# A streaming encoder step with a mixture of experts: gate and up matrices loaded whole, in rows of 16 KB, into buffers on multiples of 128 bytes

## What is computed

```
xn = rms_norm(x, norm2_g)
... router: top group of 4, then top 2 of its 8 experts; combine[n, e] are the weights
for e in range(N_EXPERTS):
    hdn = silu(xn @ w_gate[e]) * (xn @ w_up[e])       # w_gate[e], w_up[e]: 1024 x 512
    out = out + combine[:, e:e+1] * (hdn @ w_down[e])  # w_down[e]: 512 x 1024
y = rms_norm(x + out, final_norm_g)
```

## Time and profile before

| what | value |
|---|---|
| median of 3 runs | 850.46 us (848.34 to 850.73) |
| the profiled execution | 847.72 us |
| its span, first to last instruction | 845.2 us |
| PE (TensorE matmul) busy | 777.2 us, 92% |
| DVE, ACT, POOL busy | 51%, 38%, 31% |
| moved by DMA | 249.98 MB, mean 296 GB/s |
| mean granted TensorE clock | 0.981 |

### The profile page before, as it was taken

How to read it: one execution, slowest core, us unless ns; L and a number is a source line. 1 busy time by engine, 2 the same in 40 slices (tenths; PEclk the granted TensorE clock), 3 DMA queues, 4 the chain that set the end, 5 groups by cost and what they waited for, 6 DMA issues and landing times.

```text
span 845.2 us, 21580 instructions
## 1 busy us (share of the span) xinstructions
PE 777.2 (92%) x8655; PEld 593.2 (70%) x8656; DVE 427.1 (51%) x1142; ACT 323.2 (38%) x559; POOL 258.5 (31%) x129
## 2 busy tenths in 40 slices
PE   3999999999999999999999989999899879989964
PEld 3999999999999999874555555555555545555532
DVE  4046978899994334144444433445333324334424
ACT  5333666655335833152332322322323213322224
POOL 3845699978576778300000000000000000000000
PEclk9999999999999999989999999999999999999997
DMA  7734343424444845974799999999999999999993
GB/s 253 228 101 150 100 125 125 150 92 144 152 167 150 299 140 214 329 320 147 307 415 419 421 421 421 419 420 421 422 420 419 421 421 422 420 420 420 422 420 153
DMA packets 53171, 249.98 MB, mean 296 GB/s; under 512 B 6599, under 2 KB 6599, under 8 KB 28561
## 3 DMA queue, kind: packets, MB, share of 16 engines
q1 hardware_dynamic: 49760, 246.95, 74.0%
q10 hardware_dynamic: 3377, 2.57, 1.3%
HBM read 246.76 MB, written 2.75 MB: 295 GB/s over the span
## 4 chain that ended last, share of the span: by engine, by line
PE 61%; DMA 21%; DVE 11%; ACT 3%; issue 2%; SPq 1%; POOL 1%; ACTq 0%; DVEq 0%
PE bank L1402 25%; DMA piece<-in_exp_w_up 20%; PE bank L1571 12%; DVE bank L1053 7%; PE bank L1600 7%; PE bank L1522 4%; PE bank L1559 4%; PE bank L1400 4%; PE bank L1587 1%; DVE sq L1115 1%; DMA raw<-in_w_in 1%; PE bank L1529 1%; SPq L548 1%; PE bank L1469 1%; PE bank L1463 1%
## 5 line engine op out<-in xcount | busy, mean ns | idle before, releaser
L602 POOL TENSOR_TENSOR w_lo<-raw,w_hi 128x2048 fp32r<-128x2048 f32 x40 | 184.9, 4624 | 76.5 <-ACT w_hi L721 76.4
L1571 PE MATMUL bank<-piece,xe 128*32 128x256 f32 x2816 | 168.7, 391 | 32.4 <-DMA piece<-in_exp_w_up 26.4
L1571 PEld LDWEIGHTS bank<-piece,xe 128*32 128x32 f32 x2816 | 97.2, 112 | 98.2 <-issue 48.0
L1402 PE MATMUL bank<-x_hi,w_hi 128*128 128x384 f32 x448 | 152.6, 341 | 1.2 <-POOL w_lo L602 1.1
L1402 PE MATMUL bank<-x_hi,w_lo 128*128 128x384 f32 x448 | 151.0, 337 | 0.0
L1402 PE MATMUL bank<-x_lo,w_hi 128*128 128x384 f32 x448 | 150.4, 336 | 0.0
L1053 DVE SCALAR_TENSOR_TENSOR bank<-ub,vec,bank 128x256 f32<-128x256 f32 (+1 forms) x416 | 137.1, 414 | 0.0
L721 ACT ACTIVATE w_hi<-raw 128x2048 fp32r<-128x2048 f32 x40 | 76.5, 1916 | 84.1 <-PE bank L1402 72.5
L1284 DVE SCALAR_TENSOR_TENSOR silu_and_hid<-bank,small,silu_and_hid 64x256 f32<-64x256 f32 x44 | 21.5, 489 | 170.3 <-ACT silu_and_hid L902 170.3
L1600 PE MATMUL bank<-piece,hidT 128*32 128x256 f32 x1408 | 94.2, 384 | 5.4
L1402 PEld LDWEIGHTS bank<-x_hi,w_hi 128*128 128x128 f32 x448 | 83.9, 187 | 2.3 <-POOL w_lo L602 1.3
(11 more groups left out here) (231 smaller groups left out, 983.7 us busy)
## 6 DMA issues: line engine op xcount, KB each, us to landing
piece<-in_exp_w_down SPq DMA_DIRECT2D x64, 1024.0 KB, 26.7
piece<-in_exp_w_gate SPq DMA_DIRECT2D x64, 1024.0 KB, 25.9
piece<-in_exp_w_up SPq DMA_DIRECT2D x64, 1024.0 KB, 27.0
raw<-in_w_in SPq DMA_DIRECT2D x28, 1024.0 KB, 5.2
raw<-in_w_out_a SPq DMA_DIRECT2D x4, 1024.0 KB, 5.1
raw<-in_w_out_b SPq DMA_DIRECT2D x4, 1024.0 KB, 5.3
raw<-in_w_o SPq DMA_DIRECT2D x4, 1024.0 KB, 5.0
out<-n_out SPq DMA_DIRECT2D x3, 512.0 KB, 3.3
```

Of the source, the lines that this page charges most:

```text
L602: pool.tensor_tensor(w_lo[u % NW][:, :, :], raw[u % NW][:, :, :], w_hi[u % NW][:, :, :].bitcast(F32), ALU.subtract).then_inc(lo_ready, 1)
L1402: ins = pe.matmul(b, wp[:, k % UK, cols], xp[:, k, :], start=start, stop=stop)
L1571: last = pe.matmul(GU[q * T:(q + 1) * T, :], xe[:, k, :], wide(pairs[q // 2], k)[:, q % 2 * QE:(q % 2 + 1) * QE], start=(k == 0), stop=(k ...
```

## The change

Gate and up are loaded as whole matrices. `w_gu` gives partition p eight rows that follow each other, so a load is 2 MB in 128 rows of 16 KB. The contraction's blocks are cut to match: block k holds the rows with index k modulo 8 (`by_row`, `norm2_by_row`), where they were k modulo 4 within a half. `SETS` is renumbered so that the two pieces of gate and of up are neighbours with an even first number, and `matrix` names them as one buffer. Down stays in two halves.

On TensorE the two parts become one: it waits for both whole matrices, does 64 matmuls and counts up `gate_up_done`; `gate_up_half` is gone. On SP, `expert_weights` waits for `gate_up_done` once, issues the two matrices, and then down's halves as before. The first loads are re-ordered by hand for the new buffers.

`small` shrinks from 48 to 32 columns and `norm2_by_row` moves, with a few small vectors, into `few` behind `halves`. With that, `halves` begins at byte 31,488, a multiple of 128 (and of 256).

```diff
     HALF = 512
-    SETS = (((15, 16), (17, 18), (20, 9)), ((10, 11), (12, 1), (2, 0)),
-            ((4, 7), (5, 8), (3, 6)), ((13, 14), (19, 21), (22, 23)))
+    SETS = (((16, 17), (10, 11), (18, 9)), ((0, 1), (4, 5), (8, 19)),
+            ((2, 3), (6, 7), (12, 13)), ((14, 15), (20, 21), (22, 23)))
+    assert all(a % 2 == 0 and b == a + 1 for s in SETS for a, b in s[0:2])
...
         iota = sb("iota", [P, T])
-        small = sb("small", [P, 48])
-        norm2_by_row = sb("norm2_by_row", [P, KB])
-        same_at = nc.sbuf_base - 4 * (2 * KB * N + 4 * N + P + T + 48 + KB)
+        small = sb("small", [P, 32])
+        same_at = nc.sbuf_base - 4 * (2 * KB * N + 4 * N + P + T + 32)
...
         halves_at = nc.sbuf_base
+        assert halves_at % 128 == 0
         halves = sb("halves", [P, HALVES * 2048])
+        few = sb("few", [P, 24])
+        norm2_by_row, mark, zero = few[:, 0:KB], few[:, 8:14], few[0:1, 14:18]
+        own_slot, slot_coef, second_sums = few[:, 18:19], few[:, 19:20], few[:, 20:20 + NT]
...
         squares = at("squares", [P, HALF], F32, halves_at + UNIT * SETS[0][1][1])
-        assert SETS[0][0][1] == SETS[0][0][0] + 1
+        matrix = {s[c][0]: at(f"matrix{s[c][0]}", [P, 4096], F32, halves_at + UNIT * s[c][0]) for s in SETS for c in range(2)}
...
         down_rank = late("down_rank", [P, NE])[:, :]
-        mark = small[:, 36:36 + 6]
-        zero = small[0:1, 31:35]
-        own_slot = small[:, 45:46]
-        slot_coef = small[:, 46:47]
...
         xe_ready = sem("xe_ready")
-        gate_up_half = sem("gate_up_half")
...
                 "Wo": w_o.rearrange("l (k p) c -> p (l k) c", p=P)}
-        w_gu = {0: w_gate.rearrange("l e (h p j) c -> (l e) h p (j c)", h=2, p=P),
-                1: w_up.rearrange("l e (h p j) c -> (l e) h p (j c)", h=2, p=P)}
+        w_gu = {0: w_gate.rearrange("l e (p j) c -> (l e) p (j c)", p=P), 1: w_up.rearrange("l e (p j) c -> (l e) p (j c)", p=P)}
...
-        RJ = KB // 2
...
-            return t.rearrange("p (h q j) -> p h j q", h=2, q=P)
+            return t.rearrange("p (q j) -> p j q", q=P)
         def wide(pair, k):
-            return piece[pair[k // RJ]][:, :].rearrange("p (j c) -> p j c", j=RJ)[:, k % RJ, :]
+            return matrix[pair[0]][:, :].rearrange("p (k c) -> p k c", k=KB)[:, k, :]
...
-            def first_weights(e, c, h):
-                n = SETS[e][c][h]
-                sp.dma_start(piece[n][:, :], (w_dn if c == 2 else w_gu[c])[e, h]).then_inc(weights_in[n], 16)
-            TAPS_USED = {32: (0, 0), 33: (1, 0), 34: (0, 1), 35: (1, 1)}
+            def first_matrix(e, c):
+                n = SETS[e][c][0]
+                sp.dma_start(matrix[n][:, :], w_gu[c][e]).then_inc(weights_in[n], 16)
+            def first_down(e, h):
+                n = SETS[e][2][h]
+                sp.dma_start(piece[n][:, :], w_dn[e, h]).then_inc(weights_in[n], 16)
+            TAPS_USED = 32
...
             for u in range(UNITS):
-                if u == 30:
-                    first_weights(0, 2, 0)
...
                 sp.dma_start(raw[u % NW][:, :, :], w[:, k0:k0 + UK, c0:c0 + HALF]).then_inc(unit_in[u % NW], 16)
-                if u in TAPS_USED:
+                if u == TAPS_USED:
...
                     sp.wait_ge(tails_ready, 2 + 4 * KB)
-                    first_weights(0, *TAPS_USED[u])
+                    first_matrix(0, 0)
+                if u == TAPS_USED + 2:
+                    first_down(0, 0)
             sp.wait_ge(grp_done, CHUNK_END[X_LO_USED])
-            first_weights(0, 2, 1)
+            first_down(0, 1)
             sp.wait_ge(grp_done, CHUNK_END[NCH - 3])
-            first_weights(1, 0, 0)
-            first_weights(1, 0, 1)
-            first_weights(1, 1, 0)
-            sp.wait_ge(lo_ready, UNITS - 2)
-            first_weights(1, 1, 1)
-            sp.wait_ge(lo_ready, UNITS - 1)
-            first_weights(1, 2, 0)
+            first_matrix(0, 1)
             sp.wait_ge(lo_ready, UNITS)
-            first_weights(1, 2, 1)
+            first_matrix(1, 0)
             sp.wait_ge(grp_done, CHUNK_END[NCH - 2])
-            first_weights(2, 0, 0)
-            first_weights(2, 0, 1)
             sp.wait_ge(half_done, NCH)
-            first_weights(2, 1, 0)
-            first_weights(2, 1, 1)
+            first_matrix(1, 1)
+            first_down(1, 0)
             sp.wait_ge(grp_done, len(GROUPS))
-            first_weights(2, 2, 0)
-            first_weights(2, 2, 1)
-            first_weights(3, 0, 0)
-            first_weights(3, 0, 1)
+            first_matrix(2, 0)
+            first_matrix(2, 1)
+            first_down(2, 0)
+            first_down(2, 1)
+            first_matrix(3, 0)
             sp.wait_ge(aux_done, aux("logit", NT - 1) + 1)
-            first_weights(3, 1, 0)
+            first_down(1, 1)
...
             sp.wait_ge(combined, 1)
-            first_weights(3, 1, 1)
-            first_weights(3, 2, 0)
-            first_weights(3, 2, 1)
+            first_matrix(3, 1)
+            first_down(3, 0)
+            first_down(3, 1)
...
-                for c, h in ((0, 0), (1, 0), (0, 1), (1, 1), (2, 0), (2, 1)):
-                    n = SETS[side][c][h]
-                    used = (down_half, down_done) if c == 2 else (gate_up_half, gate_up_done)
-                    sp.wait_ge(used[h], last_item)
-                    src = w_dn if c == 2 else w_gu[c]
-                    sp.dma_start(piece[n][:, :], src[bass.ds(e, 1), h, :, :].rearrange("e p x -> p (e x)"))\
+                sp.wait_ge(gate_up_done, last_item)
+                for c in range(2):
+                    n = SETS[side][c][0]
+                    sp.dma_start(matrix[n][:, :], w_gu[c][bass.ds(e, 1), :, :].rearrange("e p x -> p (e x)"))\
+                      .then_inc(weights_in[n], 16)
+                for h, done in enumerate((down_half, down_done)):
+                    n = SETS[side][2][h]
+                    sp.wait_ge(done, last_item)
+                    sp.dma_start(piece[n][:, :], w_dn[bass.ds(e, 1), h, :, :].rearrange("e p x -> p (e x)"))\
...
             act.dma_start(rw[:, :, NG:R], expert_w.rearrange("l (k p) g -> p (l k) g", p=P)).then_inc(rw_in, 16)
-            act.dma_start(norm2_by_row[:, :].rearrange("p (h j) -> p h j", h=2),
-                          norm2_g.rearrange("l (h p j) -> p (l h) j", h=2, p=P)).then_inc(rw_in, 16)
+            act.dma_start(norm2_by_row, norm2_g.rearrange("l (p j) -> p (l j)", p=P)).then_inc(rw_in, 16)
...
-                act.activation(x_rows[:, i, :].rearrange("p (h j q) -> p h j q", h=2, j=RJ), by_row(x_tok[:, i, :]),
+                act.activation(x_rows[:, i, :].rearrange("p (j q) -> p j q", j=KB), by_row(x_tok[:, i, :]),
...
                     act.wait_ge(weighted, 2 * n + 1)
-                at_col = (16, 42)[h] + i
+                sums = (small[:, 16:16 + NT], second_sums)[h]
                 act.activation(squares[:, :], total(i, h)[:, :], ACT.Square, scale=1.0 / ROOT_D,
-                               accum_out=small[:, at_col:at_col + 1]).then_inc(ssq_ready, 1)
+                               accum_out=sums[:, i:i + 1]).then_inc(ssq_ready, 1)
...
                 dve.wait_ge(ssq_ready, 2 * NT + 2 * n + 2)
-                dve.scalar_tensor_tensor(small[:, 20 + i:21 + i], small[:, 16 + i:17 + i], 1e-6, small[:, 42 + i:43 + i],
+                dve.scalar_tensor_tensor(small[:, 20 + i:21 + i], small[:, 16 + i:17 + i], 1e-6, second_sums[:, i:i + 1],
...
                 pe.wait_ge(xe_ready, i + 1)
-                for part, done in enumerate((gate_up_half, gate_up_done)):
-                    pe.wait_ge(weights_in[pairs[0][part]], filled)
-                    pe.wait_ge(weights_in[pairs[1][part]], filled)
-                    for k in range(part * KB // 2, (part + 1) * KB // 2):
-                        for q in range(TILES):
-                            last = pe.matmul(GU[q * T:(q + 1) * T, :], xe[:, k, :],
-                                             wide(pairs[q // 2], k)[:, q % 2 * QE:(q % 2 + 1) * QE],
-                                             start=(k == 0), stop=(k == KB - 1))
-                    last.then_inc(done, 1)
+                pe.wait_ge(weights_in[pairs[0][0]], filled)
+                pe.wait_ge(weights_in[pairs[1][0]], filled)
+                for k in range(KB):
+                    for q in range(TILES):
+                        last = pe.matmul(GU[q * T:(q + 1) * T, :], xe[:, k, :],
+                                         wide(pairs[q // 2], k)[:, q % 2 * QE:(q % 2 + 1) * QE],
+                                         start=(k == 0), stop=(k == KB - 1))
+                last.then_inc(gate_up_done, 1)
```

## The result

The changed kernel takes **846.46 us** (median of 6 runs, 844.61 to 847.10). The kernel before, run beside it, takes 850.87 us (6 runs, 848.34 to 852.11). The ratio is 0.9947, with a 95% interval from 0.9932 to 0.9961: faster by 4.4 us, with 3.3 to 5.8 us inside the interval. The forecast was 849.6 us with a range of 841.5 to 855.5, so the time lies within the range. But it is not the likeliest case that came true: -0.9 us was forecast for it, and the result stands nearer to where rival A put it (844.6 us).

The account below looks back on a forecast made before the run. It took one full stream of expert weights from 421.07 us to the last up matrix, plus TensorE's tail, as the bound. Terms -4.9 + 1.7 + 1.5 + 0.8 = -0.9 us gave 849.6 us on the median's scale, range 841.5 to 855.5.

Parts of the forecast that it names:

- the likeliest case: Whole kernel: the forecast itself, -0.9 us in sum, 849.6 us on the scale of the medians, chance 0.43.
- rival A: Weight stream: alignment counts as well, every packet loses some 6 to 11 ns; 844.6 us, chance 0.32.
- What bounds the kernel: Second half: one unbroken stream of weights, full from 421.07 us, sets the end, followed by TensorE's work after it.
- Length of the stream, -4.9 us: Loads of 27 experts: 16 fewer packets per expert and engine, each 11.5 ns fixed, make the stream 4.9 us shorter.
- Rival B: Stream and waits: 16 KB packets run no faster and coarser waits stay, +4.9 us, 855.3 us, chance 0.20.
- The 2 KB stretch: Queue at 302 to 310 us: 87.5 ns per 2 KB packet, set against 315.6 ns at 8 KB to price packets.
- I take 0 for the alignment: Weight buffers 96 bytes past a multiple of 128: moving them was priced at 0, with -14.9 us as the bound.
- Start, +1.7 us: Second refill on SP: waiting for the whole gate-up starts the full stream 1.7 us later.
- 64 matmuls after the last landing, +1.5 us: Last item on TensorE: all 64 matmuls follow the landing, 3.45 us instead of 1.93, so +1.5 us.
- Clock, +0.8 us: Last gate-up: a 6 us wait in one piece makes a TensorE clock drop likelier, +0.8 us, bounds 0 and 3.3.
- From the profile to the median: Whole kernel: 2.7 us, the median's distance above the profiled execution, added to 846.8 us to give 849.6 us.
- Rival C, ACT's copies: Ahead of the router: token copies reading with a 32-byte step delay its chain, +3 us, 852.6 us, chance 0.05.

Follow-up runs that it names:

- e2: The changed kernel with clamped item bounds, its weight buffers put back 96 bytes past a multiple of 128; 849.88 us, ratio 1.0012 to the kernel before.
- c_before: Control: the kernel before with the item bounds that TensorE loads clamped at 0; 850.99 us, ratio 1.0020 to the kernel before.
- e1: c_before with only small tiles moved, so that the buffers begin on a multiple of 128 bytes; 846.0 us, ratio 0.9961 to the kernel before.
- e4: c_after with gate and up rows laid out for 8 KB packets, still in 2 MB loads; 850.91 us, ratio 1.0019 to the kernel before.
- c_after: Control: the changed kernel with the item bounds that TensorE loads clamped at 0; 846.63 us, ratio 0.9965 to the kernel before.
- e3: c_before with coarse waits alone, all four gate and up pieces waited for and let go together; 854.58 us, ratio 1.0049 to the kernel before.
- e5: c_after with gate and up rows laid out for 4 KB packets, still in 2 MB loads; 859.34 us, ratio 1.0115 to the kernel before.
- e6: c_after with the buffers 64 bytes past a multiple of 128; 848.39 us, ratio 0.9982 to the kernel before.
- f1: c_after with first refills of sets 0 and 1 and the last expert's gate and up by halves; 843.32 us, ratio 0.9919 to the kernel before.

## Why the prediction was right and where it failed

**What bounds the kernel: right.** One stream from the second refill to the last up matrix, then a tail. The packet experiments move the end by what they add to the stream, 3.95 us of stream for 4.3 us of time and 12.05 for 12.7.

**Length of the stream, -4.9 us: right in kind, the packets' part a little large.** The stream became 5.1 to 5.4 us shorter, but packets are only 3.6 to 4.3 us of it, 8.4 to 10.0 ns each instead of 11.5; the rest is alignment. That the total came out so near to -4.9 is luck: a price of packets that was too large stood in for an alignment that was put at 0. The 2 KB stretch overstated the price, by what wasn't tried. Rival B's extreme, 16 KB packets no faster, is refuted. But its tipping point of 9.3 ns, below which the coarse waits cost more than the packets bring, lies within what was measured: without the alignment the change would be about worth nothing, as e2 is (1.1 us under c_before, the ratios' intervals overlap). The Trainium skill (DMA: Bandwidth & Descriptors, Anatomy of one DMA, for DMAs that GpSimd issues) gives each DMA about 2 us of fixed cost; on SP's queue here e1 with 1 MB loads and e4 with 2 MB loads stream alike, so if there is such a cost the queue hid it, as the prediction took it. (The 26 us that it gives for a load in flight are 27.0 in the row that it names; nothing hangs on it.)

**"I take 0 for the alignment": this step failed.** It is worth 0.8 to 1.5 us in the stream, some 1 ns a packet, far from the bound of 11.5 ns. And it is worth 1.8 to 1.9 us in TensorE's matmuls, where the prediction didn't look at all: it treated the place of the buffers as a matter of packets, though the split weights lie behind the same tiles and move with them. By medians the two kernels with one edit each say more, 5.0 us (e1 against c_before) and 3.3 us (c_after against e2), while the rows account for 3.4 and 2.7 us (1.9 + 1.5 and 1.9 + 0.8). What remains, 1.6 and 0.6 us, is within what these comparisons can tell, and one profile a kernel doesn't settle it. Rival A was right that alignment counts as well. Its mechanism, 6 to 11 ns on every packet, was not what happened, so that its time (844.6 us) came nearer than the forecast's was luck.

**Start, +1.7 us: right.** 1.74 us between the profiles. **64 matmuls after the last landing, +1.5 us: right**; e3 pays start and end together, 3.6 us by medians and 2.5 by ratios, and there is no starvation.

**Clock, +0.8 us: not borne out by the averages.** The drop was argued from a wait of 6 us in one piece; in the changed kernel the waits came out at 3.7 and 3.9 us. In the profiled pair the tail's 3.23 us are 1.71 for the first half of the matmuls (3.64 less 1.93) and 1.5 for the clock: the drop costs 1.5 us (5.14 us against the 3.64 us that such a group takes at full clock on this timeline), and in c_after 2.7. But it is not new: c_before pays 1.7 in its last half and 1.2 in the gather behind it, e1 1.3 and 0.5. Over after, c_after, e2, e3, e4, e5 and e6 the loss is 1.9 us on average (1.5, 2.7, 1.7, 1.7, 2.5, 1.7, 1.3, all in the gate-up), over before, c_before and e1 it is 1.6 (0, 2.95, 1.8). The difference is 0.3 us, too little to tell from nothing with three executions on one side. A tail without any drop was seen in one of the three kernels that take the last gate-up by halves, in none of the seven that take it whole, and in f1, which takes it by halves.

**From the profile to the median.** I added 2.7 us to the sum, the distance of the median before from its profiled execution, as though it were a constant of the measurement. It was luck of that one execution: its tail is 2.95 us shorter than c_before's (21.27 against 24.22), all of it clock (1.71 in the half, 1.24 in the gather). On the scale of the profiles the forecast of -0.9 us is close to the -1.2 that came; on the scale of the medians it is 3.5 us off. The terms as measured add up better: -1.8 for the mixer, -5.3 for the stream, +1.7 for the later refill, and +2.0 after the last up matrix (24.85 us on average in the seven kernels with the coarse form at the end, against 22.82 in the three with the fine one) are -3.4, against -4.4 by medians. The pair of profiles hid this because in it the mixer's 1.9 us were given back before the stream began. The first items, before and then after:

```profile
391.37 4.20 PE L1571 MATMUL bank<-piece,xe 128*32 128x256 f32 x64
...
400.94 3.64 PE L1571 MATMUL bank<-piece,xe 128*32 128x256 f32 x64
```

```profile
390.62 4.94 PE L1565 MATMUL bank<-matrix,xe 128*32 128x256 f32 x64
...
400.94 3.64 PE L1565 MATMUL bank<-matrix,xe 128*32 128x256 f32 x64
```

The first gate-up starts 0.75 us earlier and takes 0.74 us longer, at lower clock, so the second one starts at the same 400.94. The other 1.2 us went in the router ahead of it. But alignment is not what does this. In e1, with the same alignment, the second gate-up starts at 398.72, and the mixer's gain is kept. From the end of the mixer to the second gate-up (by the chain) it is 36.5 to 36.7 us in before, c_before, e1 and e2, 37.2 in e6 and 38.3 to 38.8 in the other six, e3 with buffers 96 past among them. Whether that is chance of an execution or comes with the coarse form, which all of the six have in the first sets (but e2 and e6 as well), one profile a kernel doesn't show. The medians speak for chance: e3's 3.6 us are filled by the later refill and the tail (1.7 + 2.0) without it.

**Rival C, ACT's copies: refuted.** With a step of 32 bytes they take about what they took with 16, 2.12 and 2.05 us against 2.04 and 2.08. The rule of the Trainium skill (SBUF — State Buffer, Door 1) is that each access to a new 16-byte line pays; with four-byte elements 16 and 32 bytes are alike in this. The trace agrees, and so does e5, whose step of 8 bytes has two elements in each line and takes 1.11 us. After, and then e5:

```profile
362.09 2.12 ACT L863 ACTIVATE x_rows<-x_tok 128x1024 f32<-128x1024 f32 x1
...
366.69 2.05 ACT L863 ACTIVATE x_rows<-x_tok 128x1024 f32<-128x1024 f32 x1
```

```profile
361.78 1.11 ACT L867 ACTIVATE x_rows<-x_tok 128x1024 f32<-128x1024 f32 x1
```

## What to carry to other kernels

Before pricing a moved buffer, list every engine that reads it, and not only the queue that fills it: here an effect nearly as large as that of the packets (2.6 to 3.4 us against 3.6 to 4.3 by the rows) was an alignment that no line of the loads showed. It was to be had with a few small tiles moved and nothing else. Larger packets save a fixed sum each. Coarser waits cost at the two ends of the stream, where nothing hides them; take the coarse form in the middle and keep the fine one for the first refill and the last. A profiled execution that is faster than all the timed ones is no base for a sum until it is known which of its waits or clock levels were lucky.

## What the runs showed of the hardware beyond the forecast

- TensorE's matmuls (fp32r) can depend on where the split weights lie in SBUF. With 384 columns moving and the weights stationary, 540 take 94.5 us with buffers 96 bytes past a multiple of 128, 93.9 on a multiple, 94.1 at 64. With the weights moving (512 columns), 144 take 33.31, 32.70 and 33.01 us. But 192 others, on weights in the same buffers, take 33.5 us in all three.
- For transfers into SBUF, 96 past costs about 1 ns a packet, at 8 and at 16 KB; 64 past costs nothing that the queue shows (153.02 MB against 153.03 in 360 us).
- A packet costs about 9 ns beside its bytes, 9.4 from 4 to 8 KB and 9.1 from 8 to 16 KB; the rates are 413, 421 and 425 GB/s, with down's packets at 8 KB throughout.
- Whether TensorE's clock drops at a gate-up after a wait differs between executions: the same 32 matmuls took 1.93 us in before and 3.64 in c_before, which has one more register instruction for each bound, after the same wait of 3.05 us. Over the whole execution, the runs of the kernel before itself have mean granted clocks from 0.971 to 0.981.
